# The triangular inverse of the rwkv scan on 32x32 diagonal blocks, four array tiles in turn

## The reference, cut to what matters

```python
def _rwkv7_step(state, inp):
    r_t, w_t, k_t, v_t, a_t, b_t = inp
    sa = jnp.einsum('bhvk,bhk->bhv', state, a_t)
    state = (state * w_t[:, :, None, :] + sa[..., None] * b_t[:, :, None, :]
             + v_t[..., None] * k_t[:, :, None, :])
    return state, jnp.einsum('bhvk,bhk->bhv', state, r_t)
```

## Time and profile before

| | us |
|---|---|
| median of 3 runs | 1252.81 |
| lowest and highest run | 1251.59, 1252.86 |
| span of the profiled execution | 1250.2 |
| PE busy in the span | 1231.39 (98%) |
| PEld busy | 1078.01 |
| DVE busy | 531.34 |
| ACT busy | 607.91 |
| POOL busy | 766.72 |
| inverse of pass 0, first level_x to first level_x of pass 1 | 943.4 to 979.4 |
| inverse of pass 1, to the end of the solve of its first chunk | 979.4 to 1015.3 |

### The profile page before, as it was taken

The page is one execution under the profiler, slowest core; times in us unless marked ns, Lnnn a source line. Parts: engine busy times, 40 slices in busy tenths (PEclk is TensorE's granted clock), DMA queues, the critical chain, the costliest instruction groups (busy, mean ns, idle before and its releaser), DMA issues.

```text
span 1250.2 us, 22958 instructions
## 1 busy us (share of the span) xinstructions
PE 1231.4 (98%) x9568; PEld 1078.0 (86%) x9568; DVE 531.3 (43%) x818; ACT 607.9 (49%) x793; POOL 766.7 (61%) x194
## 2 busy tenths in 40 slices
PE   8999999999999999999999999999999999999998
PEld 7888887888988888899998888878888998888887
DVE  4233234755333233342533223354968735423333
ACT  7455444445554544584655444432332455644442
POOL 3988870262378888676379888800035325788885
PEclk9999999999999999999999999999999999999999
DMA  7655554244345555644246555523442013555552
GB/s 299 217 180 192 201 179 145 94 169 140 126 157 200 187 201 183 207 174 161 76 159 213 181 189 201 181 100 123 140 171 96 4 38 107 191 201 179 198 194 74
DMA packets 30587, 200.79 MB, mean 161 GB/s; under 512 B 3376, under 2 KB 5296, under 8 KB 6832
## 3 DMA queue, kind: packets, MB, share of 16 engines
q1 hardware_dynamic: 27776, 195.43, 44.4%
q10 hardware_dynamic: 2736, 4.26, 1.0%
HBM read 197.58 MB, written 2.10 MB: 160 GB/s over the span
## 4 chain that ended last, share of the span: by engine, by line
PE 91%; DVE 4%; ACT 2%; issue 1%; POOL 1%; DMA 1%; SPq 0%; POOLq 0%; DVEq 0%
PE psum L340 25%; PE psum L342 13%; PE psum L331 10%; PE psum L333 10%; PE psum L332 9%; PE psum L973 8%; PE psum L986 3%; POOL wlo L3189 1%; PE psum L2724 1%; PE psum L2835 1%; PE psum L2851 1%; PE psum L328 1%; PE psum L586 1%; PE psum L329 1%; PE psum L330 1%
## 5 line engine op out<-in xcount | busy, mean ns | idle before, releaser
L3189 POOL TENSOR_TENSOR wlo<-raw,whi 128x2048 fp32r<-128x2048 f32 x158 | 726.9, 4605 | 375.7 <-ACT whi L301 358.6
L340 PE MATMUL psum<-f_both,whi 128*128 128x512 f32 x1408 | 492.2, 393 | 1.3 <-DVE wlo L686 1.3
L301 ACT ACTIVATE whi<-raw 128x2048 fp32r<-128x2048 f32 x157 | 300.6, 1915 | 226.9 <-PE psum L342 169.4
L342 PE MATMUL psum<-f_both,wlo 128*128 128x256 f32 x1408 | 393.9, 280 | 0.0
L340 PEld LDWEIGHTS psum<-f_both,whi 128*128 128x128 f32 x1408 | 264.4, 188 | 60.0 <-DVE wlo L686 1.9
L342 PEld LDWEIGHTS psum<-f_both,wlo 128*128 128x128 f32 x1408 | 264.6, 188 | 1.5
L331 PE MATMUL psum<-whi,ahi 128*128 128x512 f32 x352 | 137.5, 391 | 0.3 <-POOL wlo L3189 0.3
L333 PE MATMUL psum<-whi,alo 128*128 128x512 f32 x352 | 137.1, 390 | 0.0
L332 PE MATMUL psum<-wlo,ahi 128*128 128x512 f32 x352 | 137.0, 389 | 0.0
L896 DVE TENSOR_TENSOR psum<-psum,arena 128x512 f32<-128x512 f32 x43 | 30.1, 699 | 241.8 <-ACT arena L612 241.7
L331 PE MATMUL psum<-whi,hhi 128*128 128x256 f32 x368 | 106.6, 290 | 2.6 <-DVE hlo L2687 1.2
(11 more groups left out here) (397 smaller groups left out, 1421.9 us busy)
## 6 DMA issues: line engine op xcount, KB each, us to landing
raw<-stream SPq DMA_DIRECT2D x182, 1024.0 KB, 4.9
con<-consts SPq DMA_DIRECT2D x1, 1216.0 KB, 13.6
x<-x_in SPq DMA_DIRECT2D x1, 1024.0 KB, 5.0
raw<-stream SPq DMA_DIRECT2D x2, 512.0 KB, 6.8
kept_x<-x ACTq DMA_DIRECT2D x1, 1024.0 KB, 5.9
x<-kept_x ACTq DMA_DIRECT2D x1, 1024.0 KB, 4.8
out<-x SPq DMA_DIRECT2D x4, 256.0 KB, 2.0
arena<-gm_w_s ACTq DMA_DIRECT2D x1, 512.0 KB
```

What stands on the lines that cost most here:

```text
L301: nc.scalar.activation(whi[:, slot, :], raw[:, c % RAW, :], ACT.Copy).then_inc(high_made, 1)
L340: nc.tensor.matmul(psum[:, bank, :].rearrange("p (a n) -> p a n", a=2), whi[w], f_both[:, :, k, :], start=k == 0, stop=False, skip_group_c ...
L342: return nc.tensor.matmul(psum[:, bank, 0:TOK], wlo[w], f_hi[:, k, :], start=False, stop=k == KT - 1, skip_group_check=True)
L3189: nc.gpsimd.tensor_tensor(part(wlo[:, slot, :]), part(raw[:, c % RAW, :]), part(whi[:, slot, :]).bitcast(F32), ALU.subtract)\
```

## The change

The inverse is now built on the four 32x32 diagonal blocks of the 128 partitions alone. In a tile of a half, each head keeps only 32 columns: the rows of partition quarter i hold its diagonal block i. So T, T', X and the masked L are 128x256 where they were 128x512. `start_turned` first masks L to these blocks (`near`, still 128x512), folds the two column halves into one by an addition (`LT_block`), and masks that for the 2x2 start. Levels 0 to 3 (s = 2 to 16) run on the blocks: each group is 32 products of 32x32 by 32x32, one for each head and quarter, on four array tiles in turn, (0,0), (32,32), (64,64) and (96,96).

The last level (s = 32) makes the block that lies off the diagonal between the two diagonal blocks of a chunk. It is one product off the diagonal in `level_x`, and one in `level_t`, for each head and chunk, so 16 products a group, on two 32x32 tiles. The whole T' (`TT_whole`, 128x512) that `u_solve` reads is then put together. POOL spreads the diagonal blocks and writes zeros beside them (`diagonal_blocks`, two instructions of 128x512 a pass, in the place of the mask of the last level), and DVE copies the block off the diagonal out of PSUM (two copies of 32 partitions x 256 for each half, where one addition of 128x512 was). The constants that are loaded at the start have 320 more columns. The rename of `rw_kk` changes nothing in the timing; the semaphore also counts `LT_block` now.

```diff
+    local, own = i[:, 0:32], j % 32
+    parts["near"] = (within // 32 == down // 32) & (down < within)
+    parts["block"] = within // 32 == down // 32
+    parts["block_ident"] = local == own
+    for s in (1, 2, 4, 8, 16):
+        parts[f"block{s}"] = (local // (2 * s) == own // (2 * s)) & ((local // s) % 2 == 1) & ((own // s) % 2 == 0)
...
-        T_half = [area(12288 + 512 * q, 8, 64) for q in range(2)]
-        TTr_half = [[area(13312 + 512 * q, 8, 64) for q in range(2)],
+        T_block = [area(12288 + 256 * q, 8, 32) for q in range(2)]
+        TT_block = [[area(at + 256 * q, 8, 32) for q in range(2)] for at in (12800, MORE_AT + 1536)]
+        TT_whole = [[area(13312 + 512 * q, 8, 64) for q in range(2)],
                     [area(MORE_AT + 2048 + 512 * q, 8, 64) for q in range(2)]]
-        X_half = [area(MORE_AT + 1024 + 512 * q, 8, 64) for q in range(2)]
+        X_block = [area(MORE_AT + 1024 + 256 * q, 8, 32) for q in range(2)]
...
-        LT_level = [area(20480 + 512 * q, 8, 64) for q in range(2)]
+        LT_level, LT_block = ([area(at + 256 * q, 8, 32) for q in range(2)] for at in (20480, 20992))
+        block_sums = lambda q: psum[:, q, 0:256].rearrange("p (e n) -> p e n", e=8)
+        QUARTERS = [slice(32 * i_, 32 * i_ + 32) for i_ in range(4)]
...
-                    nc.scalar.activation(X_half[q], bank8(q), ACT.Copy).then_inc(s("rw_x"), 1)
+                    nc.scalar.activation(X_block[q], block_sums(q), ACT.Copy).then_inc(s("rw_x"), 1)
...
+            def start_turned(m, q, decays):
+
+                apart = TT_whole[m][q]
+                steps(nc.vector.tensor_tensor(apart, decays, over8("near"), ALU.mult))
+                if m:
+                    eng.wait_ge(s("rw_level_masked"), 5 + q)
+                nc.vector.tensor_tensor(LT_block[q], apart[:, :, 0:32], apart[:, :, 32:64], ALU.add).then_inc(s("rw_kk_near"), 1)
+                eng.wait_ge(s("rw_kk_near"), 8 + 2 * m + q + 1)
+                steps(nc.vector.tensor_tensor(TT_block[m][q], LT_block[q], blocks8("block1"), ALU.mult))
+                steps(nc.vector.tensor_tensor(TT_block[m][q], blocks8("block_ident"), TT_block[m][q], ALU.add))
...
-                steps(nc.vector.tensor_tensor(TTr_half[0][q], decays, over8("half1"), ALU.mult))
-                nc.vector.tensor_tensor(LT_level[q], decays, over8("half2"), ALU.mult)
-                steps(nc.vector.tensor_tensor(TTr_half[0][q], over8("half_ident"), TTr_half[0][q], ALU.add))
+                start_turned(0, q, psum[:, 2 + 2 * q:4 + 2 * q, :].rearrange("p b (a n) -> p (b a) n", a=4)[:, :, 0:64])
+                nc.vector.tensor_tensor(LT_level[q], LT_block[q], blocks8("block2"), ALU.mult)
...
+            def second_start(q):
+
+                eng.wait_ge(s("rw_masked"), 8 + 2 * q + 2)
+                start_turned(1, q, LR[1][q][:, :, 0:64])
...
                 if n == len(LEVELS) - 1:
-                    nc.vector.tensor_tensor(TTr_half[m][q], TTr_half[m][q], bank8(q), ALU.add).then_inc(s("rw_tnew"), 1)
+                    eng.wait_ge(s("rw_level_masked"), 10 * m + 6 + q + 1)
+                    for first in (QUARTERS[0], QUARTERS[2]):
+                        ins = nc.vector.tensor_copy(TT_whole[m][q][first, :, 32:64], block_sums(q)[first, :, :])
+                    ins.then_inc(s("rw_tnew"), 1)
                 else:
-                    nc.vector.tensor_tensor(T_half[q], T_half[q], bank8(q), ALU.add).then_inc(s("rw_tnew"), 1)
+                    nc.vector.tensor_tensor(T_block[q], T_block[q], block_sums(q), ALU.add).then_inc(s("rw_tnew"), 1)
                     eng.wait_ge(s("rw_tnew"), at_level(m, n, q) + 1)
-                    nc.vector.transpose(TTr_half[m][q].rearrange("p e n -> p (e n)"),
-                                        T_half[q].rearrange("p e n -> p (e n)")).then_inc(s("rw_tturned"), 1)
+                    nc.vector.transpose(flat(TT_block[m][q]), flat(T_block[q])).then_inc(s("rw_tturned"), 1)
...
-                    if m or n:
-                        eng.wait_ge(s("rw_level_masked"), at_level(m, n, q) - 1)
-                    for e in range(8):
-                        for c in range(2):
-                            r = slice(64 * c, 64 * c + 64)
-                            mm = nc.tensor.matmul(bank8(q)[r, e, :], LT_level[q][r, e, :], T_half[q][r, e, :], start=True, stop=True)
+                    if n == len(LEVELS) - 1:
+                        eng.wait_ge(s("rw_masked"), 8 * m + 2 * q + 2)
+                        for e in range(8):
+                            for c in range(2):
+                                r = QUARTERS[2 * c]
+                                mm = nc.tensor.matmul(block_sums(q)[QUARTERS[2 * c + 1], e, :], LR[m][q][r, e, 32:64], T_block[q][r, e, :],
+                                                      start=True, stop=True, tile_position=(64 * c, 64 * c + 32))
+                    else:
+                        if m or n:
+                            eng.wait_ge(s("rw_level_masked"), (8 * m if m else -2) + 2 * n + q + 1)
+                        for e in range(8):
+                            for at, r in enumerate(QUARTERS):
+                                mm = nc.tensor.matmul(block_sums(q)[r, e, :], LT_level[q][r, e, :], T_block[q][r, e, :], start=True, stop=True,
+                                                      tile_position=(32 * at, 32 * at))
...
-                    for e in range(8):
-                        for c in range(2):
-                            r = slice(64 * c, 64 * c + 64)
-                            if n == len(LEVELS) - 1:
-                                mm = nc.tensor.matmul(bank8(q)[r, e, :], X_half[q][r, e, :], TTr_half[m][q][r, e, :],
-                                                      start=True, stop=True)
-                            else:
-                                mm = nc.tensor.matmul(bank8(q)[r, e, :], TTr_half[m][q][r, e, :], X_half[q][r, e, :],
-                                                      start=True, stop=True)
+                    if n == len(LEVELS) - 1:
+                        for e in range(8):
+                            for c in range(2):
+                                r = QUARTERS[2 * c + 1]
+                                mm = nc.tensor.matmul(block_sums(q)[QUARTERS[2 * c], e, :], X_block[q][r, e, :], TT_block[m][q][r, e, :],
+                                                      start=True, stop=True, tile_position=(64 * c + 32, 64 * c))
+                    else:
+                        for e in range(8):
+                            for at, r in enumerate(QUARTERS):
+                                mm = nc.tensor.matmul(block_sums(q)[r, e, :], TT_block[m][q][r, e, :], X_block[q][r, e, :], start=True, stop=True,
+                                                      tile_position=(32 * at, 32 * at))
...
+                over = const(f"block{LEVELS[n]}", 32).rearrange("p (a n) -> p a n", a=1).broadcast_to((P, 8, 32))
                 for q in range(2):
-                    eng.wait_ge(s("rw_masked"), 8 * m + 2 * q + 2)
+                    eng.wait_ge(s("rw_kk_near"), 8 + 2 * m + q + 1)
                     eng.wait_ge(s("rw_xsum"), at_level(m, n, q) - 1)
-                    nc.gpsimd.tensor_tensor(LT_level[q], LR[m][q][:, :, 0:64], over8, ALU.mult)\
+                    nc.gpsimd.tensor_tensor(LT_level[q], LT_block[q], over, ALU.mult).then_inc(s("rw_level_masked"), 1)
+
+            def diagonal_blocks(m):
+
+                apart = const("block", 64).rearrange("p (a b n) -> p a b n", a=1, b=2).broadcast_to((P, 8, 2, 32))
+                for q in range(2):
+                    eng.wait_ge(s("rw_tturned"), 10 * m + 2 * (len(LEVELS) - 1) + q + 1)
+                    nc.gpsimd.tensor_tensor(TT_whole[m][q].rearrange("p e (b n) -> p e b n", b=2),
+                                            TT_block[m][q].rearrange("p e (b n) -> p e b n", b=1).broadcast_to((P, 8, 2, 32)), apart, ALU.mult)\
...
-            for n_ in range(1, len(LEVELS)):
+            for n_ in range(1, len(LEVELS) - 1):
                 level_mask(0, n_)
                 if n_ < 3:
                     to_tokens(1, n_ - 1)
-            for n_ in range(len(LEVELS)):
+            diagonal_blocks(0)
+            for n_ in range(len(LEVELS) - 1):
                 level_mask(1, n_)
                 if n_ == 2:
                     decayed(1)
+            diagonal_blocks(1)
```

19 lines of the change are left out of this document (7 added, 12 removed).

## The result

The changed kernel takes 1280.33 us in the median of 4 runs (1277.33 to 1282.65), where the kernel before, beside it on the same chip, took 1252.7. The ratio is 1.0222, with a 95% interval of 1.021 to 1.0234: slower by 27.6 us. I had forecast 15 us slower and a range up to 1275. The direction held, and so did what bounds the two passes; the size didn't, and the time lies outside the range.

A forecast was written before the change was run, and what follows sets the result against it. PE's instruction supply, 3.4 us a block, was taken to bound the inverse's two passes: +7 us in pass 0 and +9.5 in pass 1, +16.5 rounded to +15. So 1252.8 + 15 = 1268 us, range 1245 to 1275.

The forecast's parts named there:

- What bounds the kernel: In the inverse's two passes, PE is bound by its instruction supply, 3.4 us a block of some 250; chance 0.52.
- the one stop of 1.4 us: Pass 0, 955.70 to 957.13: PE stops inside a group whose inputs are there, read as a late instruction block.
- Array time: Groups of levels 0 to 3: 0.92 us falls to 0.46, a gain taken as 0.5 us a group.
- the shorter DVE work: Additions and transposes of the levels fall by some 0.25 us each, 8 us of DVE, 4 in each pass.
- Rival 1: Both passes: blocks can come in about 2.1 us, so the array gain arrives; -8, 1245 us (1241 to 1248); chance 0.24.
- Rival 3: Level groups: each record needs 26 to 29 ns on the array whatever its tile; +13 and +8, 1273 us; chance 0.10.
- Rival 2: Both passes: a middle fetch time, 2.6 to 3.0 us a block; -2 to +7, 1250 to 1261 us; chance 0.14.
- the price of a block: Both passes: fetching one block of PE instructions takes 3.4 us, from packets 3.45 us apart; 8.2 blocks are added.
- the clock: Named as a failure case: long stops might lower the granted clock from 1.00, doubling array time; nothing in the sum.
- my 1.5: Pass 1: 47.0 us becomes 45.5, as a block and a third loads during the starting wait and the end runs at array speed.
- The late block: Pass 0, `level_x` of level 1: PE runs dry at about 952.5 until about 956.7, when the block behind the weights comes.
- The 30 changes of array shape: Both passes (13 and 17): switches between 32x32 and 64x64 groups, 0.15 us each, 4.5 us, hidden below the supply.

The follow-up runs named there:

- Experiment 3: The kernel before, each 64x64 product of all five levels cut into two of 64x32, 10 instruction blocks more: 1283.56 us, ratio 1.0249.
- experiment 1: The changed kernel with products of only four of eight heads in levels 0 to 3, so the PE instructions of the kernel before: 1253.65 us, ratio 1.0012.
- experiment 8: The kernel before with 512 idle 32x32 products on four tiles behind the last product of all, 8 instruction blocks: 1276.67 us, ratio 1.0192.
- experiment 4: The kernel before with only the last level done as two 32x32 products off the diagonal, no PE instruction added: 1254.4 us, ratio 1.0017.
- experiment 9: The changed kernel with one idle 128x512 product ahead of each of the 8 groups of pass 1's last two levels: 1283.61 us, ratio 1.0244.
- experiment 2: The changed kernel with products of six of eight heads in levels 0 to 3, 4 instruction blocks more than before: 1266.59 us, ratio 1.0102.
- experiment 5: The changed kernel with one idle 128x512 product ahead of each group of levels 0 to 3: 1284.23 us.
- experiments 10 and 11: The kernel before with 36 and with 20 tiny idle products at its start, moving the borders of the instruction blocks: 1252.14 and 1251.58 us.

## Why the prediction was right in direction and wrong in size

**What bounds the kernel** was read rightly: the one stop of 1.4 us and the even packets of the earlier trace rows were the sign. Experiment 3 adds instructions at the old array time and is 31 us slower; experiment 1 keeps the new tiles without the added instructions and costs 1 us; experiment 8 shows the wait with nothing else beside it.

**Array time** came as forecast (0.5 us a group at full clock), and so did the shorter DVE work. In the changed kernel both lie inside the waits, and experiment 4 shows for the last level of the kernel before that the shorter array time had no taker. Rival 1 needed a block in 2.1 us; it takes 3.75. Rival 3, a price per record of 26 ns, falls with the 8.6 ns. Rival 2, a block in 2.6 to 3.0 us, falls with experiment 8. The Trainium skill, Runtime: NRT & Kernel Launch, Instruction fetch mechanics, has the block right, 256 instructions, but not that its cost is mostly hidden: 2.46 of the 3.74 us from 1251.16 to 1254.90 in experiment 8 are waited for.

**Two steps failed: the price of a block, and the clock, which I put at nothing.** By place, in the profiled executions:

| | forecast | measured |
|---|---|---|
| first `level_x` of pass 1 later by | 7 | 11.8 |
| from there to the end of the first chunk's solve, longer by | 9.5 | 15.4 |
| from there to the last solve, longer by | 0 | 2.2 |

So 13 us were missing in the spans.

**The price of a block.** I took 3.4 us from the four packets of the earlier trace rows and noted that there was "never a shorter one". That makes it the minimum, and I used it as the mean. In pass 0 the 6.2 blocks from the late one to the end of level 3 took 22.3 us for the 21 of my sum. In pass 1 I had counted 250 instructions to a block, which makes 13.8 blocks; with the 256 of experiment 8 they are 13.5, and at 3.75 us, less my 1.5, they give 49.1 us for 45.5. Together this is some 5 of the 13 us. The rounding from 16.5 down to 15, "since some fetches may be quicker", went the same wrong way: hardly one was.

**The clock** I had named as a thing that would make the prediction wrong, and left out of the sum. After the first long stops it fell, from 1.00 before 958 to 0.7 to 0.8 on the mean. Where PE waits for blocks that costs little (experiments 3 and 8); where it is a full queue it costs all of it. That is 16 records of `turn` at 980.58 in 3.67 us, where 8 take 1.09 at full clock, so some 1.5 us ahead of pass 1. And it is the 4.5 us behind the last `level_t` (experiment 9), of which about half stand in the second row of the table and 2.2 us in the third. Together this is 6 of the 13 us. With the price alone put right the forecast would have been 1274, inside the range; the clock takes the time out of it.

**The late block** came 1.6 us later than I had said, 958.3 for 956.7, for a reason that no run shows. Of PE's 3.6 us of waiting there, 1.8 are the ordinary wait, since it came 5.6 us after the block ahead of it. Some 0.5 us are left over, and 1.1 us by which pass 0 itself begins later stand in the first row; its cause I didn't look for. The median differs by less than the profiled execution, 27.6 for 29.2. The runs of the changed kernel spread over 5.3 us, those of experiment 3 with its nearly full clock over 2.8. In experiments 1, 2 and 5 the longer runs are mostly those with the lower clock, which speaks for the clock as the cause of the spread, but no run tests it.

**The 30 changes of array shape**, which I priced at 4.5 us and hid beneath the supply, lie inside the waits of the changed kernel, and what they cost there can't be told. Their single price was right: experiment 4 shows 0.16 us for one between 64x64 and 32x32.

No kernel here beats the one before and computes the whole. The runs point at one way, fewer PE instructions for the same products. That wasn't tried.

## What to carry to other kernels

Count PE's instructions before you cut a product into smaller tiles. In all shapes of this case a float32 product costs four of them, two matmuls and two weight loads, and 256 of them take 3.75 us to arrive, 14.6 ns each. A group is bound by the larger of its array time and that, and here 64x64 products of 14.4 ns an instruction already stood at the edge. Look for short stops put down to "issue" inside a group, and for the packets of the instruction queue: where these stood evenly at their smallest spacing, as here, the kernel was near that edge, and a shorter array time brought nothing (experiment 4). And a price read from the trace as "never less than" is a bound, not a mean.

## What the runs showed of the hardware

- Where PE waited for its instructions, a block of 256 came every 3.47 to 4.03 us, 3.75 on the mean, with no other transfer running (experiment 8), and 3.63 and 3.75 on the mean in the two passes of the changed kernel.
- 32x32 float32 products on four tiles in turn start 8.6 ns apart, over three times as fast as 64x64 products on two (28.8 ns).
- Once PE waited at nearly every block, for 0.2 to 2.1 us and once 3.6, the granted clock was 0.71 on the mean from 958 to 1047 us, which is half speed (1.2 of 2.4 GHz) for over half of that time. In experiment 3, whose waits are of the same kind between longer array work, it was 0.96 and 0.97. One wait of 2.96 us went ahead of a clock of 0.61 over the next 4.4 us (experiment 4).
- For a block that fell due beside a burst of the weight stream PE waited 1.4 us in the kernel before, 3.6 in the changed one, and with other borders of the blocks 0.8 us and not at all (experiments 10 and 11).
